# Moving operand sums and a reload in the order of two MLP layers

## What is computed

```
f = sq_relu_mlp(rmsnorm_2(x, g[2]), w_mlp_up[i], w_mlp_down[i])
x = x + rmsnorm_2(f, g[3])
gate = jax.nn.sigmoid(rmsnorm_2(x, g[4]) @ w_ple_gate[i])
e = (p[i] @ w_ple_proj[i]) * gate

def sq_relu_mlp(h, w_up, w_down):
    return jnp.square(jax.nn.relu(h @ w_up)) @ w_down
```

## Time and profile before

| | |
|---|---|
| median of three runs | 1716.07 us |
| the profiled execution's own time | 1716.07 us |
| its span (first to last instruction) | 1714.3 us |
| mean granted TensorE clock | 0.996 |
| PE busy | 99% |
| DVE, ACT, POOL busy | 74%, 56%, 10% |
| DMA | 177.52 MB, mean 104 GB/s |

### The profile page before, as it was taken

The page is one execution under the profiler, slowest core; times in us unless marked ns, Lnnn a source line. Parts: engine busy times, 40 slices in busy tenths (PEclk is TensorE's granted clock), DMA queues, the critical chain, the costliest instruction groups (busy, mean ns, idle before and its releaser), DMA issues.

```text
span 1714.3 us, 25289 instructions
## 1 busy us (share of the span) xinstructions
PE 1689.9 (99%) x9375; PEld 1460.7 (85%) x9375; DVE 1272.0 (74%) x2020; ACT 957.0 (56%) x1645; POOL 169.7 (10%) x147
## 2 busy tenths in 40 slices
PE   9999999999999999999999999999999999999998
PEld 7888877888788897789899998878887889999977
DVE  6378877776567777588698996785566968898966
ACT  4267875665426666477546464642235766464655
POOL 2011212000300000220000002420003000000041
PEclk9999999999999999999999999999999999999999
DMA  8222124214242222243232443313323432323621
GB/s 274 81 72 74 43 75 100 72 50 147 74 112 75 74 75 80 74 172 121 77 123 77 147 162 121 111 56 111 104 88 103 157 108 99 99 99 99 233 75 50
DMA packets 152786, 177.52 MB, mean 104 GB/s; under 512 B 18281, under 2 KB 126342, under 8 KB 150886
## 3 DMA queue, kind: packets, MB, share of 16 engines
q1 hardware_dynamic: 150790, 159.22, 29.4%
q10 hardware_dynamic: 1888, 16.85, 2.5%
HBM read 158.82 MB, written 12.58 MB: 100 GB/s over the span
## 4 chain that ended last, share of the span: by engine, by line
PE 93%; DVE 4%; ACT 2%; issue 1%; DVEq 0%; ACTq 0%
PE bank L1158 28%; PE bank L1159 28%; PE bank L1160 28%; PE bank L1507 2%; PE bank L1531 1%; PE bank L1426 1%; DVE split_weights L2671 1%; PE bank L1415 1%; DVE act_a L2673 0%; PE bank L1823 0%; ACT act_a L1920 0%; DVE work L2706 0%; PE bank L1341 0%; DVE act_b L2671 0%; PE bank L1325 0%
## 5 line engine op out<-in xcount | busy, mean ns | idle before, releaser
L1158 PE MATMUL bank<-act_a,split_weights 128*128 128x512 f32 (+1 forms) x1360 | 525.3, 386 | 6.3 <-DVE act_a L2671 2.0
L1160 PE MATMUL bank<-act_a,split_weights 128*128 128x512 f32 (+1 forms) x1360 | 518.7, 381 | 0.0
L1159 PE MATMUL bank<-act_a,split_weights 128*128 128x512 f32 (+1 forms) x1360 | 518.2, 381 | 0.0
L1158 PEld LDWEIGHTS bank<-act_a,split_weights 128*128 128x128 f32 x1360 | 255.9, 188 | 58.5 <-issue 6.1
L1160 PEld LDWEIGHTS bank<-act_a,split_weights 128*128 128x128 f32 x1360 | 255.7, 188 | 50.1
L1159 PEld LDWEIGHTS bank<-act_a,split_weights 128*128 128x128 f32 x1360 | 256.0, 188 | 45.2 <-issue 0.2
L1158 PE MATMUL bank<-act_b,split_weights 128*128 128x256 f32 (+1 forms) x648 | 208.3, 321 | 4.1 <-ACT work L2391 4.0
L1160 PE MATMUL bank<-act_b,split_weights 128*128 128x256 f32 (+1 forms) x648 | 207.1, 320 | 0.0
L1159 PE MATMUL bank<-act_b,split_weights 128*128 128x256 f32 (+1 forms) x648 | 207.0, 319 | 0.0
L2613 DVE TENSOR_TENSOR split_weights<-raw_weights,split_weights 128x2048 fp32r<-128x2048 f32 x55 | 127.1, 2310 | 76.2 <-ACT split_weights L1865 63.2
L1865 ACT ACTIVATE split_weights<-raw_weights 128x2048 fp32r<-128x2048 f32 x51 | 97.3, 1908 | 119.5 <-PE bank L1160 119.5
(11 more groups left out here) (356 smaller groups left out, 3259.2 us busy)
## 6 DMA issues: line engine op xcount, KB each, us to landing
raw_weights<-in_w_mlp_up SPq DMA_DIRECT2D x32, 1024.0 KB, 5.4
raw_weights<-in_w_mlp_down SPq DMA_DIRECT2D x32, 1024.0 KB, 5.3
raw_weights<-in_w_in SPq DMA_DIRECT2D x18, 1024.0 KB, 5.2
raw_weights<-in_w_conv_in SPq DMA_DIRECT2D x12, 1024.0 KB, 5.1
raw_weights<-in_w_attn_in SPq DMA_DIRECT2D x16, 512.0 KB, 5.2
raw_weights<-in_w_ple_gate SPq DMA_DIRECT2D x8, 1024.0 KB, 5.0
raw_weights<-in_w_out SPq DMA_DIRECT2D x4, 1024.0 KB, 5.2
raw_weights<-in_w_attn_in SPq DMA_DIRECT2D x4, 1024.0 KB, 5.4
```

Source lines behind the costliest of these rows:

```text
L1158: nc.tensor.matmul(dst, w[0], a[0], start=first, stop=False)
L1159: nc.tensor.matmul(dst, w[0], a[1], start=False, stop=False)
L1160: mm = nc.tensor.matmul(dst, w[1], a[0], start=False, stop=last)
```

## The change

The change rewrites the order strings. In the first chunk the steps X, Q and H move from the stretch of p4 to p19 into that of p19 to n2, on ACT and on DVE; in the fourth chunk B0 moves from behind s2 to behind p13. The order on PE, SP and POOL is as before, and no instruction is added or removed (ACT_PLAIN and DVE_PLAIN are names for the front of the first chunk's strings). Of the diff, the lines on ACT:

```
-        ACT_MLP = ("s0 b0 t0 v0 U3 s1 b1 t1 v1 p0 p1 p2 p3 s2 b2 t2 v2 X0 p4 p5 H0 p6 p7 s3 b3 p8 t3 p9 v3 X1 p10 p11 H1 p12 p13 "
-                   "X2 p14 p15 H2 a0 p16 a1 p17 X3 a2 p18 a3 p19 H3 a4 p20 a5 p21 a6 p22 p23 p24 p25 p26 "
-                   "p27 a7 n0 a8 a9 n1 a10 n2 a11 a12 a13 n3",
+        ACT_MLP = ("s0 b0 t0 v0 " + ACT_PLAIN + "p14 p15 a0 p16 a1 p17 a2 p18 X0 a3 p19 a4 H0 p20 a5 p21 a6 X1 p22 p23 p24 H1 p25 p26 "
+                   "p27 a7 n0 X2 a8 H2 a9 n1 X3 a10 H3 n2 a11 a12 a13 n3",
...
-                   ACT_THIRD.replace("s2 b2", "s2 B0 b2") + "k0 c0 c1 c2 j0 q0 q1 q2 q3 n0 q4 q5 q6 q7")
+                   ACT_THIRD + "B0 k0 c0 c1 c2 j0 q0 q1 q2 q3 n0 q4 q5 q6 q7")
```

and on DVE the first chunk's tail, from S2 on:

```
-                   "Q1 p10 p11 H1 p12 p13 S2 Q2 p14 p15 H2 p16 z2 p17 Q3 p18 p19 H3 p20 S3 p21 p22 p23 z3 p24 p25 p26 p27 n0 n1 n2 n3",
+        DVE_MLP = (DVE_PLAIN + "S2 p14 p15 p16 z2 p17 p18 p19 Q0 p20 H0 S3 p21 p22 Q1 p23 z3 p24 p25 H1 p26 p27 n0 Q2 H2 n1 Q3 H3 n2 n3",
```

More of the change, by code:

```diff
@@ L765, in up_unit_number @@
             return 4 * MLP_CHUNKS * layer + 4 * c + u
+        ACT_PLAIN = "U3 s1 b1 t1 v1 p0 p1 p2 p3 s2 b2 t2 v2 p4 p5 p6 p7 s3 b3 p8 t3 p9 v3 p10 p11 p12 p13 "
         ACT_THIRD = ("g14 g15 s0 b0 t0 g16 v0 g17 s1 b1 g18 t1 g19 v1 g20 o2 N6 N7 p0 p1 p2 p3 s2 b2 t2 v2 "
                      "p4 p5 p6 p7 s3 b3 p8 t3 p9 v3 p10 p11 p12 p13 ")
-        ACT_MLP = ("s0 b0 t0 v0 U3 s1 b1 t1 v1 p0 p1 p2 p3 s2 b2 t2 v2 X0 p4 p5 H0 p6 p7 s3 b3 p8 t3 p9 v3 X1 p10 p11 H1 p12 p13 "
-                   "X2 p14 p15 H2 a0 p16 a1 p17 X3 a2 p18 a3 p19 H3 a4 p20 a5 p21 a6 p22 p23 p24 p25 p26 "
-                   "p27 a7 n0 a8 a9 n1 a10 n2 a11 a12 a13 n3",
+        ACT_MLP = ("s0 b0 t0 v0 " + ACT_PLAIN + "p14 p15 a0 p16 a1 p17 a2 p18 X0 a3 p19 a4 H0 p20 a5 p21 a6 X1 p22 p23 p24 H1 p25 p26 "
+                   "p27 a7 n0 X2 a8 H2 a9 n1 X3 a10 H3 n2 a11 a12 a13 n3",
                    ACT_THIRD + "p14 p15 p16 p17 p18 p19 p20 p21 p22 p23 p24 p25 p26 p27 i0 i1 i2 i3",
                    "i4 i5 i6 o0 N2 N3 " + ACT_THIRD + "p14 p15 p16 p17 p18 p19 p20 p21 p22 p23 p24 p25 p26 p27 n0 n1 n2 n3",
-                   ACT_THIRD.replace("s2 b2", "s2 B0 b2") + "k0 c0 c1 c2 j0 q0 q1 q2 q3 n0 q4 q5 q6 q7")
+                   ACT_THIRD + "B0 k0 c0 c1 c2 j0 q0 q1 q2 q3 n0 q4 q5 q6 q7")
+        DVE_PLAIN = ("T0 b0 y0 t0 v0 U3 T1 b1 y1 t1 v1 S0 p0 p1 p2 z0 p3 T2 b2 y2 t2 v2 p4 p5 p6 S1 p7 T3 b3 y3 p8 t3 p9 v3 z1 "
+                     "p10 p11 p12 p13 ")
         DVE_THIRD = ("g14 g15 T0 b0 y0 t0 g16 v0 g17 F2 T1 b1 g18 y1 t1 g19 v1 g20 N6 N7 d8 d9 d10 S0 p0 d11 p1 p2 z0 p3 "
@@ L777, in hybrid_block_kernel @@
         DVE_DOWN = "S2 p14 p15 a0 p16 a1 z2 p17 a2 p18 a3 p19 a4 p20 a5 S3 p21 a6 p22 p23 z3 p24 p25 p26 p27 "
-        DVE_MLP = ("T0 b0 y0 t0 v0 U3 T1 b1 y1 t1 v1 S0 p0 p1 p2 z0 p3 T2 b2 y2 t2 v2 Q0 p4 p5 H0 p6 S1 p7 T3 b3 y3 p8 t3 p9 v3 z1 "
-                   "Q1 p10 p11 H1 p12 p13 S2 Q2 p14 p15 H2 p16 z2 p17 Q3 p18 p19 H3 p20 S3 p21 p22 p23 z3 p24 p25 p26 p27 n0 n1 n2 n3",
+        DVE_MLP = (DVE_PLAIN + "S2 p14 p15 p16 z2 p17 p18 p19 Q0 p20 H0 S3 p21 p22 Q1 p23 z3 p24 p25 H1 p26 p27 n0 Q2 H2 n1 Q3 H3 n2 n3",
                    "G2 " + DVE_THIRD + DVE_DOWN + "I0 a7 i0 a8 i1 i2 a9 i3 K0",
```

## The result

The changed kernel takes 1731.4 us, median of 4 runs (1730.2 to 1733.0), beside 1716.2 for the kernel before (4 runs, 1715.2 to 1716.4). The ratio is 1.0091, 95% interval 1.0073 to 1.0108: slower by 0.9%. The forecast was 1726 with a range from 1718 to 1730.5; the sign was right, and the time lies above the range. The profiled execution took 1730.9 us, with a span of 1729.1.

A forecast was written before the change was run, and what follows sets the result against it. PE is busy 99% of the span, so only its few waits can give or cost time. 1716.1 - 1.7 + 1.2 + 8.6 + 2.5 = 1726.7; forecast time 1726 us, range 1718 to 1730.5.

The forecast's parts named there:

- first chunk, without the clock: First chunk up to u0 of the second: gain of 0.4 us in layer 0 and 1.3 in layer 1, sum 1.7.
- slow clock behind the u0 waits: Behind PE's new wait at u0, TensorE's slow clock may come again: 1.2 us added for both layers.
- unit 31 and the statistics: Fourth chunk: late weight load makes PE wait and the statistics late, 4.3 us lost per layer, 8.6 in all.
- slow clock behind the late waits: Fourth chunk: PE idles about 3 us and slow clock may follow, 1.25 us added a layer, 2.5 in the sum.
- the old wait: PE at d2 of the first chunk, waiting for bank copies aK: 2.0 us once in each layer, claimed to go.
- the chain n0, Q2, H2, a9, n1: Serial DVE and ACT steps ahead of u0, second chunk: claimed a new PE wait of 2.4 us, u0 at 811.6.
- L: Time when unit 31's weight load lands in the fourth chunk: taken as 1047.4; it costs from 1043.1 on.
- the fifth: Share of the bytes that SP's weight load (q1) gets beside ACT's reload (q10): 0.32 MB against 1.27, 20%.
- Rival (1): Engines share by bytes, no collision in the fourth chunk, first chunk as forecast: 1715.6 us, chance 0.12.
- (2): Both sides good, no collision in the fourth chunk and no new wait at u0: 1709.5 us, chance 0.06.
- (3): Collision in the fourth chunk, but the first chunk gives its full 6.6 us: 1720.6 us, chance 0.07.
- Rival (4): Reloads hold back SP's load wholly, landing at 1048.7 or later, slow clock behind each wait: 1730 us, chance 0.07.

The follow-up runs named there:

- run 4: The change with the reload at its old place and the sums' last two rounds (X, H, Q) put behind n1: 1709.3 us, ratio 0.9953.
- run 1: The kernel before with only the reload moved to its late place, behind p13 of the fourth chunk: 1728.3 us, ratio 1.0067.
- run 5: The change with the reload moved one place further, behind c2 on ACT: 1726.4 us, ratio 1.0060.
- run 7: The change with half of the reload (e and p, 2 MB) back at its old place and x (2 MB) late: 1718.4 us, ratio 1.0005.
- run 10: The changed kernel once more, unaltered, for a second look at its clock: 1730.1 us, one run.
- run 2: The change with the reload back at its old place, so only the sums (X, Q, H) are moved: 1718.0 us, ratio 1.0008.
- run 6: The change with l7 put ahead of c2 in DVE's order of the last chunk: 1726.6 us, ratio 1.0056.

## Why the prediction was partly wrong, step by step

| step | forecast, us | measured in the trace, us |
|---|---|---|
| first chunk, without the clock | -1.7 | -0.75 |
| slow clock behind the u0 waits | +1.2 | +3.0 |
| unit 31 and the statistics | +8.6 | +9.3 |
| slow clock behind the late waits | +2.5 | +3.7 |
| sum | +10.6 | +15.2 (with -0.3 elsewhere: 14.9) |

(The refill of 0.13 behind each u0 wait is in the first line, not in the clock's.)

**What held.** That the old wait goes in both layers; that the chain n0, Q2, H2, a9, n1 brings a new one at u0, of 2.64 us (forecast 2.4) and at the time forecast, shown by run 4, which breaks the chain and gets the whole 6.6; that the reload slows the load of unit 31 to 13 to 15 us (13.5 and 14.0), shown by runs 1, 5 and 7 (L was taken from the stash at the layer's start, in which q1 waited in the same way, so it came out although the fifth was not the whole story); L, the wait of 1.0 at unit 31 (1.0 in layer 0, 1.2 in layer 1) and the second statistics product at L + 20.0. Rival (1), bytes shared equally, falls with the 13.5 us here and the 13.7 of run 1: the load got less than its share, not more. Rivals (2) and (3) fall with the wait at u0.

**What failed.** The two terms for the clock. The step was: "One of two old waits was followed by slow clock, so the 1.5 us (11.57 - 10.03) that I booked as gone in layer 1 may come again in either layer: I add 1.2 for the pair", and for the statistics "once of twice; I add 1.25 a layer". All four new waits were followed by it in the profiled execution, the last one by 6.8 us of it. The two terms came to 6.7 where I had 3.7, which is 3.0 of the 4.6 us between the sums. Over all twelve profiles of this case: of 16 waits in which PE stood for 2.3 us between two starts (the old copies' and the one at 666 us) 9 had a slow stretch behind them; of 26 of 2.4 to 3.7 us (u0 and the statistics) 20 had. Two cases were too few to take a half from: at 20 in 26 with about 1.6 us each the four waits cost 4.9, not 3.7. This alone would have moved the forecast to 1728. That the longer waits are the likelier ones to be followed isn't shown, since 9 of 16 and 20 of 26 lie within chance of each other. Nor do the terms follow from their own words: half of twice 1.5 is 1.5 and not 1.2, and 1.25 a layer has no row. The price of 1.5 was right by luck. Of the 1.54 us that d2 took longer in layer 1, 0.71 was lost in layer 0 too, where no slow clock stood, so that stretch cost 0.8 us; the ones behind u0 cost 1.4 to 1.6.

Behind it stands a second, smaller error, in the range. Its top, 1730.5, came from one bad end at a time (L late, or slow clock behind each wait). All four slow stretches as they were, with everything else as forecast, is already 1729.7. Rival (4), which is meant to hold both bad ends, was put at 1730, but its own terms add up to more: 1716.1 - 1.7 + 11.2 (twice 5.6) and 1.5 behind each of four waits is 1731.6. Half of its condition came true (slow clock behind each wait, with L as forecast), and the range should have held its sum. (The first three chances add up to 0.82, not 0.81.) The small misses in the other terms then sufficed to pass the top: 1.0 in the first chunk (layer 0 gained 0.1 and not 0.4, layer 1 0.9 and not 1.3, and each u0 wait has 0.13 of refill behind it) and 0.7 in the fourth, nearly all of it in layer 1, where unit 31 took 14.0 us. That all four stretches came in the profiled execution was not certain, as run 10 with three of them shows.

**What stays open.** What decides in a single execution whether the clock falls behind a wait of this length; run 10 shows that it isn't the kernel's order, and the wait at 666 us only that it goes with when the clock first rose. And why behind the statistics of layer 1 in the first profile the slow stretch was 6.8 us and in run 10, behind the same wait of PE, 3.4.

## What to carry to other kernels

Price each new wait of TensorE as the wait and what its clock does behind it, and take the chance from as many waits of that length as the traces have. A bulk transfer moved to where nobody waits for it still delays the load that is issued right after it, in the change and in run 7 until 1 to 2.5 us after the bulk itself had landed: look for that load's consumer, and for what stands behind the consumer in its queue. When work is moved out of the way of one product, ask which product its new neighbours feed: putting two rounds of sums behind one half unit, not ahead of it, turned 1718.0 us (run 2) into 1709.3 (run 4), from no difference to 0.5% faster, with the reload left in its place.

## What the runs showed of the hardware

- Slow clock followed 29 of 42 waits of PE with 2.3 to 3.7 us between two starts, and none that was filled with products of no use; each stretch was 3.4 us long (twice 6.8), and a single one cost 1.2 to 1.75 us, but 0.8 where PE would have lost time anyway (d2 in layer 1 of the kernel before). The same wait of the same kernel had it in one execution and not in another. Behind the wait at 666 us it came in the seven profiles whose clock first rose within 5.6 us of the span's start and in none of the five in which it rose later.
- A weight load of 1 MB that takes 5.0 to 5.3 us alone took 8.9 behind 2 MB of another queue's reload and 13.5 to 15.4 behind 4 MB, at both places tried. It got next to nothing while the other queue moved packets of about 16 KB (0.00 MB in the 3.7 us from its issue), and a fifth to a quarter of the bytes, in packets of 2 KB, beside packets of about 7 KB.
- POOL's three adds of 128x512 took 4.96 us where DVE worked beside the first of them and 4.16 where it idled, the add ahead of them 1.86 for 1.47, and DVE's 128x1024 step 2.31 for 1.22. This took away 1.2 of the 2.1 us that run 6 should have gained at the statistics.
